# Sample attention of a two-layer decode step: rounds of four column tiles instead of pairs of three

## What is computed

```python
qa = partial_rotary(heads(aq, ATT_HEADS), pos)
k_all = jnp.concatenate([k_past, ka.astype(k_past.dtype)], axis=1)
v_all = jnp.concatenate([v_past, heads(av, ATT_HEADS).astype(v_past.dtype)], axis=1)
o_a = dilated_window_attention(qa, k_all, v_all, k_past.shape[1]).reshape(B, T, -1)
...
k_buf = k_all[:, L - new_len:]
v_buf = v_all[:, L - new_len:]
```

## Time and profile before

| | before |
|---|---|
| median of the runs | 1862.29 us |
| profiled execution | 1861.73 us |
| its span | 1859.9 us |
| PE matmul records | 1780.8 us, 96% of the span |
| VectorE, ScalarE | 46%, 35% |
| mean granted clock of PE | 0.971 |
| attention stage, layer 0 (290.0 to 386.1 us) | 96.1 us, PE 84.57 us busy, DMA share 0.89 |
| attention stage, layer 1 (1212.1 to 1307.2 us) | 95.1 us, PE 84.26 us busy, DMA share 0.89 |

### The profile page before, as it was taken

One profiled execution on the slowest core, in us unless ns is written; L12 is line 12 of the kernel. 1 busy time (PEld: TensorE's weight loads), 2 busy tenths in 40 slices (PEclk: granted clock), 3 DMA queues, 4 the chain that ended last, 5 costly groups with the idle time before them and its releaser, 6 DMA issues.

```text
span 1859.9 us, 35744 instructions
## 1 busy us (share of the span) xinstructions
PE 1780.8 (96%) x16096; PEld 1651.1 (89%) x16096; DVE 863.1 (46%) x1333; ACT 655.8 (35%) x967; POOL 71.0 (4%) x90
## 2 busy tenths in 40 slices
PE   6999998999999999999989999988999999999998
PEld 5988995588999999999979889855989999999988
DVE  5514775445423333345655148854354133333465
ACT  5422324544423222233344322255344231222233
POOL 0012110000000000000000121100000000000000
PEclk9999898999999999999989998989999999999999
DMA  6521418952755626352353223289319366355311
GB/s 262 184 68 54 167 43 330 342 182 80 249 173 198 239 80 225 107 189 80 104 188 124 69 100 110 113 324 341 140 58 331 110 215 218 108 195 178 123 63 63
DMA packets 73960, 303.50 MB, mean 163 GB/s; under 512 B 6096, under 2 KB 28240, under 8 KB 72144
## 3 DMA queue, kind: packets, MB, share of 16 engines
q1 hardware_dynamic: 66384, 200.94, 30.8%
q0 software_dynamic: 7424, 100.27, 15.4%
HBM read 290.57 MB, written 110.89 MB: 216 GB/s over the span
## 4 chain that ended last, share of the span: by engine, by line
PE 89%; DVE 6%; ACT 3%; issue 1%; DMA 0%; DVEq 0%; ACTq 0%
PE pair L1651 15%; PE pair L1653 14%; PE pair L1652 14%; PE pair L864 3%; PE pair L715 3%; PE pair L717 2%; PE pair L719 2%; PE pair L990 2%; PE pair L697 2%; PE pair L647 2%; PE pair L699 2%; PE pair L698 2%; PE pair L970 2%; PE pair L649 2%; PE pair L648 2%; PE pair L1731 2%
## 5 line engine op out<-in xcount | busy, mean ns | idle before, releaser
L1651 PE MATMUL pair<-x_hi_part,w_hi_part 128*128 128x288 f32 x1088 | 322.2, 296 | 2.1 <-DVE tmp L2030 2.1
L1652 PE MATMUL pair<-x_lo_part,w_hi_part 128*128 128x288 f32 x1088 | 321.0, 295 | 0.0
L1653 PE MATMUL pair<-x_hi_part,w_lo_part 128*128 128x288 f32 x1088 | 319.9, 294 | 0.0
L1967 DVE TENSOR_TENSOR w_lo_part<-raw,w_hi_part 128x1024 fp32r<-128x1024 f32 x154 | 188.7, 1226 | 235.6 <-ACT w_hi_part L1818 235.6
L1651 PE MATMUL pair<-u_hi_part,w_hi_part 128*128 128x288 f32 x928 | 274.7, 296 | 0.0
L1652 PE MATMUL pair<-u_lo_part,w_hi_part 128*128 128x288 f32 x928 | 273.8, 295 | 0.0
L1653 PE MATMUL pair<-u_hi_part,w_lo_part 128*128 128x288 f32 x928 | 272.8, 294 | 0.0
L1818 ACT ACTIVATE w_hi_part<-raw 128x1024 fp32r<-128x1024 f32 x154 | 161.8, 1051 | 209.9 <-PE pair L1653 208.3
L1651 PEld LDWEIGHTS pair<-x_hi_part,w_hi_part 128*128 128x128 f32 x1088 | 203.9, 187 | 2.5 <-DVE tmp L2030 2.5
L1653 PEld LDWEIGHTS pair<-x_hi_part,w_lo_part 128*128 128x128 f32 x1088 | 204.9, 188 | 0.0
L1652 PEld LDWEIGHTS pair<-x_lo_part,w_hi_part 128*128 128x128 f32 x1088 | 204.3, 188 | 0.0
(11 more groups left out here) (278 smaller groups left out, 3450.8 us busy)
## 6 DMA issues: line engine op xcount, KB each, us to landing
raw<-w_units SPq DMA_DIRECT2D x210, 512.0 KB, 3.6
ck_out<-ck POOLq DMA_DIRECT2D x16, 3060.0 KB, 14.2
cv_out<-cv POOLq DMA_DIRECT2D x16, 3060.0 KB, 23.2
arena<-cv SPq DMA_DIRECT2D x8, 1920.0 KB, 13.4
tail<-cv SPq DMA_DIRECT2D x8, 1920.0 KB, 10.6
arena<-ck SPq DMA_DIRECT2D x6, 1920.0 KB, 11.7
more<-ck SPq DMA_DIRECT2D x6, 1920.0 KB, 12.1
h<-ck SPq DMA_DIRECT2D x4, 1920.0 KB, 12.2
```

Source lines behind the costliest of these rows:

```text
L1651: nc.tensor.matmul(out, wh[:, cols], xh[:, k, t], start=n == 0, stop=False)
L1652: nc.tensor.matmul(out, wh[:, cols], xl[:, k, t], start=False, stop=False)
L1653: mm = nc.tensor.matmul(out, wl[:, cols], xh[:, k, t], start=False, stop=n == KT - 1)
L1967: return tt_(dst, src, hi.bitcast(F32), ALU.subtract).then_inc(*up(done, 1))
```

## The change

The 12 combinations of a pair of batches and a pair of heads are worked off in three rounds of four column tiles instead of four rounds (pairs) of three, so that 128 rows are filled. Combination 4r + t belongs to pair (4r + t) // 3 and heads (4r + t) mod 3. There are now 12 couples = 3 rounds x 4 slots: slot 0 the output's and the round's transposes (128 columns each), slot 1 both score calls of the next round, slot 2 the first weighing, slot 3 the second. Keys and values are loaded in pieces of one batch and one pair of heads (640 KB), 24 of each, into nine and six buffers. Key piece n waits for score call (n - 9) // 4 + 1, value piece n for weighing (n - 6) // 4 + 1. In SP's order all keys come ahead of value piece 6. Values are laid out in DRAM so that a partition's ten rows of a piece are one run of 5120 bytes; before, a run was 1536 bytes. ScalarE copies the round's transposes in three instructions instead of two; VectorE's copies of the turned output stay four per round. On VectorE and ScalarE `s_max` and `s_exp` of the next round stay in slot 2. The new-position bias has three blocks instead of four. The copy of the value cache to its output takes whole rows of a batch.

```diff
-ROWS = 96
+ROUNDS, ACROSS = 3, 4
+QCOLS = 96
 COLS = KEYS + NEW
+def combination(r, t):
+    return divmod(ACROSS * r + t, 3)
+def piece(n):
+    r, j, t = n // (2 * ACROSS), n // ACROSS % 2, n % ACROSS
+    p, c = combination(r, t)
+    return 2 * p + j, c
+PIECES = 2 * ACROSS * ROUNDS
+KBUF, VBUF = 9, 6
...
-            KB = [area(0, 3 * KEYS, 3), more_sb[:, 0:3 * KEYS].rearrange("p (a t) -> p a t", a=3),
-                  h_sb[:, 0:3 * KEYS].rearrange("p (a t) -> p a t", a=3)]
-            VB = [area(16640, KC * 384, KC), area(9728, KC * 384, KC)]
-            PTB = area(13568, 11 * ROWS, 11)
-            PTP = [area(14624, 512), area(15136, 512)]
+            KB = [v[:, i * KEYS:(i + 1) * KEYS] for v in (arena, more_sb, h_sb) for i in range(3)]
+            VB = [area(o + i * KEYS, KEYS, KC) for o in (9728, 16640) for i in range(3)]
+            PTB = area(13568, 11 * P, 11)
+            PTP = [area(14976, 512), area(21824, 512)]
...
-                def load_keys(b):
-                    sp.dma_start(KB[b % 3], of_layer(ck)[b * 384:(b + 1) * 384, 0:KEYS]
-                                 .rearrange("(c p) n -> p c n", p=P)).then_inc(*up(k_landed[b % 3], 16))
-                def load_values(b):
-                    sp.dma_start(VB[b % 2], of_layer(cv)[b * WIN:b * WIN + KEYS, :]
-                                 .rearrange("(c p) n -> p c n", p=P)).then_inc(*up(v_landed[b % 2], 16))
+                def load_keys(n):
+                    b, c = piece(n)
+                    if n >= KBUF:
+                        sp.wait_ge(*at(ss_mm, (n - KBUF) // ACROSS + 1))
+                    sp.dma_start(KB[n % KBUF], of_layer(ck)[b * 384 + c * P:b * 384 + (c + 1) * P, 0:KEYS]
+                                 ).then_inc(*up(k_landed[n % KBUF], 16))
+                def load_values(n):
+                    b, c = piece(n)
+                    if n >= VBUF:
+                        sp.wait_ge(*at(so_mm, (n - VBUF) // ACROSS + 1))
+                    at_ = (3 * b + c) * WIN
+                    sp.dma_start(VB[n % VBUF].rearrange("p k n -> p (k n)"), of_layer(cv)[at_:at_ + KEYS, :]
+                                 .rearrange("(p k) n -> p (k n)", p=P)).then_inc(*up(v_landed[n % VBUF], 16))
                 sp.wait_ge(*at(lv_ready, len(LEVELS) - 1))
-                load_keys(0)
+                for n in range(3):
+                    load_keys(n)
                 sp.wait_ge(*at(lin_mm, Q[IN2[-1]] + 1))
-                load_keys(1)
-                load_keys(2)
+                for n in range(3, 9):
+                    load_keys(n)
                 sp.wait_ge(*at(lv_mm, len(LEVELS) * len(GROUPS)))
-                load_values(1)
+                for n in range(3):
+                    load_values(n)
                 sp.wait_ge(*at(o_ready, 5))
-                load_values(0)
-                def more_keys(b):
-                    sp.wait_ge(*at(ss_mm, b - 2))
-                    load_keys(b)
-                def more_values(b):
-                    sp.wait_ge(*at(so_mm, b - 1))
-                    load_values(b)
-                for b in (3, 4, 5, 6):
-                    more_keys(b)
-                more_values(2)
-                more_values(3)
-                more_keys(7)
+                for n in range(3, 6):
+                    load_values(n)
+                for n in range(9, 16):
+                    load_keys(n)
+                for n in range(16, PIECES):
+                    load_keys(n)
+                for n in range(6, 10):
+                    load_values(n)
+                for n in range(10, 14):
+                    load_values(n)
                 for r in range(R_OUT, R_OUT + AHEAD):
                     load(sp, r)
-                more_values(4)
-                more_values(5)
+                for n in range(14, 18):
+                    load_values(n)
                 for r in range(R_OUT + AHEAD, R_OUT + RAW):
                     load(sp, r)
...
+                for n in range(18, PIECES):
+                    load_values(n)
...
-                    b = 2 * p + j
-                    pe.wait_ge(*at(k_landed[b % 3], 16 * (b // 3 + 1)))
+                    first = (2 * r + j) * ACROSS
+                    for t in range(ACROSS):
+                        pe.wait_ge(*at(k_landed[(first + t) % KBUF], 16 * ((first + t) // KBUF + 1)))
                     for n, (lo, w) in enumerate(((0, 512), (512, 512), (1024, 256))):
-                        for c in range(3):
-                            mm = nc.tensor.matmul(bank[n][32 * c:32 * c + 32, 0:w], QB[:, b, c, :], KB[b % 3][:, c, lo:lo + w],
-                                             start=j == 0, stop=j == 1)
+                        for t in range(ACROSS):
+                            b, c = piece(first + t)
+                            mm = nc.tensor.matmul(bank[n][32 * t:32 * t + 32, 0:w], QB[:, b, c, :],
+                                                  KB[(first + t) % KBUF][:, lo:lo + w], start=j == 0, stop=j == 1)
                     mm.then_inc(*up(ss_mm, 1))
+                def s_turn(r):
+                    pe.wait_ge(*at(ss_exp, r + 1))
+                    if r >= 1:
+                        pe.wait_ge(*at(os_ev, r))
                     for k in range(KC):
-                        nc.tensor.transpose(bank[2 + k // 5][:, ROWS * (k % 5):ROWS * (k % 5 + 1)],
-                                            SMS[0:ROWS, k * P:(k + 1) * P], IDENT[0:ROWS, 0:ROWS])
-                    nc.tensor.transpose(bank[0][0:NEW, 0:ROWS], SMS[0:ROWS, KEYS:COLS],
-                                        IDENT[0:ROWS, 0:ROWS]).then_inc(*up(sp_mm, 1))
-                def s_weigh(p):
-                    pe.wait_ge(*at(sp_ev, p + 1))
+                        b_, o = (bank[2 + k // 4], P * (k % 4)) if k < 8 else (bank[0], P * (k - 8))
+                        nc.tensor.transpose(b_[:, o:o + P], SMS[:, k * P:(k + 1) * P], IDENT)
+                    nc.tensor.transpose(bank[0][0:NEW, 2 * P:3 * P], SMS[:, KEYS:COLS], IDENT).then_inc(*up(sp_mm, 1))
+                def s_weigh(r, j):
+                    if j == 0:
+                        pe.wait_ge(*at(sp_ev, r + 1))
+                    first = (2 * r + j) * ACROSS
+                    for t in range(ACROSS):
+                        pe.wait_ge(*at(v_landed[(first + t) % VBUF], 16 * ((first + t) // VBUF + 1)))
+                    for k in range(KC):
+                        for t in range(ACROSS):
+                            nc.tensor.matmul(bank[3][32 * t:32 * t + 32, P * j:P * j + P], PTB[:, k, 32 * t:32 * t + 32],
+                                             VB[(first + t) % VBUF][:, k, :], start=k == 0, stop=False)
+                    for t in range(ACROSS):
+                        c = combination(r, t)[1]
+                        mm = nc.tensor.matmul(bank[3][32 * t:32 * t + 32, P * j:P * j + P],
+                                              PTB[0:NEW, KC, 32 * t:32 * t + 32],
+                                              V[0:NEW, TT, 640 + P * c:640 + P * c + P], start=False, stop=True)
+                    mm.then_inc(*up(so_mm, 1))
...
                             s_back(p - 1)
                         s_turn(p)
                     elif slot == 1:
-                        if p + 1 < PAIRS:
+                        if p + 1 < ROUNDS:
                             s_scores(p + 1, 0)
                             s_scores(p + 1, 1)
+                    elif slot == 2:
+                        s_weigh(p, 0)
                     else:
-                        s_weigh(p)
+                        s_weigh(p, 1)
                 weigh(len(COUPLES) - 1)
-                s_back(PAIRS - 1)
+                s_back(ROUNDS - 1)
...
                 def s_turned(p):
                     act.wait_ge(*at(sp_mm, p + 1))
-                    A(PTB[:, 0:KC].rearrange("p (a k) m -> p a (k m)", a=2), pair[1][:, :, 0:5 * ROWS], ACT.Copy)
-                    A(PTB[0:NEW, KC], bank[0][0:NEW, 0:ROWS], ACT.Copy).then_inc(*up(sp_ev, 1))
+                    A(PTB[:, 0:8].rearrange("p (a k) m -> p a (k m)", a=2), pair[1][:, :, :], ACT.Copy)
+                    A(PTB[:, 8:KC].rearrange("p k m -> p (k m)"), bank[0][:, 0:2 * P], ACT.Copy)
+                    A(PTB[0:NEW, KC], bank[0][0:NEW, 2 * P:3 * P], ACT.Copy).then_inc(*up(sp_ev, 1))
...
```

More of the change, by code:

```diff
@@ L121 @@
 C_NBIAS = C_SBIAS + KEYS
-C_SCALE = C_NBIAS + PAIRS * NEW
+C_SCALE = C_NBIAS + ROUNDS * NEW
 C_EPS = C_SCALE + 1
@@ L289, in build @@
         pt_mm, pt_ev = sem("pt_mm"), sem("pt_ev")
-        k_landed, v_landed = [[sem(f"{n}_landed{i}") for i in range(m)] for n, m in (("k", 3), ("v", 2))]
+        k_landed, v_landed = [[sem(f"{n}_landed{i}") for i in range(m)] for n, m in (("k", KBUF), ("v", VBUF))]
         ss_mm, ss_max, ss_exp, ss_p = sem("ss_mm"), sem("ss_max"), sem("ss_exp"), sem("ss_p")
@@ L570, in _ @@
                 sp.dma_start(of_layer(kn_out).rearrange("p (c t) -> p c t", c=3), qk[:, 3:6, SEQ:T]).then_inc(*up(kv_out, 16))
-                for j in range(2):
```

(16 more changed lines are left out.)

115 lines of the change are left out of this document (52 added, 63 removed).

## The result

The changed kernel takes 1907.8 us (median of four runs, 1904.6 to 1911.9), the kernel before beside it 1863.4. The ratio is 1.0235, 95% interval 1.0211 to 1.0259; in a second comparison it was 1.0212 (1.0174 to 1.0249). The forecast of 1882 us had the direction right and somewhat under half the size (+20.5 us where +44.4 were measured), and the measured time lies above its range, which ends at 1897. The profiled execution took 1909.5 us, span 1907.7.

A forecast was written before the change was run, and what follows sets the result against it. PE's matmul work was taken as the bound. Per layer -10.1 + 12.8 + 3.2 + 4.8 = +10.7 us; two layers +21.4, less 0.9 for "issue", gave +20.5 on 1861.7: 1882 us, range 1864 to 1897.

The forecast's parts named there:

- PE's work: Attention stage, per layer: two fewer score calls and weighings, less new-key scoring, slightly cheaper transposes; -10.1 us.
- waits for values: Before each round's second weighing, PE waits for two value pieces whose buffers free late; three waits, +12.8 us per layer.
- lower clock: After each value wait PE works at 1.2 GHz, losing 2.6 us each; net +4.8 us per layer.
- The fourth column tile: Score and weighing calls: four tiles cost what three did, 2.15 and 2.66 us a call.
- the rival wanted 2.7 us or more for four: Fourth tile not free: calls up to 4/3 as long, 1901 us at most, half of it 1892; chance 0.1.
- The wait of round 0: Second weighing of round 0: values queue behind seven key pieces, landing at 332.3 us; PE waits 5.4 us.
- The waits of rounds 1 and 2: Second weighings there: two pieces land in 5.6 us, PE has 2.2 and 1.6 us of work; waits 3.4 and 4.0 us.
- Chain waits: PE's waits for ScalarE and VectorE by prompt couple, 9.3 us before and 12.5 after; +3.2 us per layer.
- The replay: PE, ScalarE, VectorE and queue replayed in program order with trace durations; kernel before ended at 385.8 us, trace 386.1.
- The clock didn't hold: Judges the rival that value waits bring no lower-clock loss afterwards: +2.8 us per layer, 1866 us; chance 0.12.
- the rival with a chance of 0.1: Small pieces land late: each value wait 1 us longer, +3 us per layer, 1888 us; chance 0.1.
- faster, the value waits are hidden: Value pieces land before PE asks for them: -6.9 us per layer, 1847 us; chance 0.07.

The follow-up runs named there:

- the kernel with the slots set anew: Changed kernel, p_out before s_turned, value pieces 6-9 before keys 17-23, first weighing in slot 1, next round's scores in slot 2; 1857.7 us, ratio 0.9962.
- the first pair of profiles: First profiled executions, nothing further changed: kernel before 1861.73 us, changed kernel 1909.5 us.
- second pair of profiles: Both kernels profiled once more, nothing further changed: changed kernel 1900.3 us, kernel before 1855.8 us.
- The kernel before with the pieces alone: Kernel before, with keys and values in three transfers per sample, the new DRAM layout of values and its copy to the output; 1869.3 us, ratio 1.0033.
- the layout alone: Kernel before, with the new DRAM layout of values and its copy to the output, but one large transfer per sample as before; 1864.3 us, ratio 0.9994.

## Why the prediction was wrong

Per layer, against the windows above. The measured share of PE's work is taken from the kernel with the slots set anew, layer 0, as its clock is that of before; the clock's share is what is left of busy time. Both columns are of the first pair of profiles.

| Term | Forecast | Layer 0 | Layer 1 |
|---|---|---|---|
| PE's work | -10.1 | -10.5 | -9.8 |
| waits for values | +12.8 | +16.2 | +16.2 |
| other waits | +3.2 | +3.8 | +6.7 |
| lower clock | +4.8 | +9.8 | +4.7 |
| stage | +10.7 | +19.3 | +17.8 |

Other waits are idle time (+20.0 and +22.9) less 16.2; the profile has no other waits for values than the six, 32.4 us in both layers. In the second pair of profiles the stages are 15.9 and 19.2 us longer and idle time 21.4 and 20.4, so a single entry for idle or busy time is good to some 4 us.

**The fourth column tile, and what PE is relieved of: right.** 2.15 and 2.67 us a call with four tiles. The Trainium skill ("TensorE: Matmul & The Clock Gate", Part 3) has a speed-up of 2.38 for three tiles. No run here has a call of one tile to hold that against; but the rival wanted 2.7 us or more for four, and the measured 2.15 us decide against it.

**The wait of round 0: mis-sized, 7.0 instead of 5.4 us.** PE came 0.6 us later than reckoned, at 329.1 instead of 328.5 (the forecast's 326.9, by its own terms 326.8, and the 1.6 us by which the stage starts later). The nine pieces took longer: from the first key issue of slot 1 to the landing 336.05 - 317.34 = 18.7 us, where 14.4 + 2.5 = 16.9 were reckoned. The mechanism, seven key pieces ahead of two value pieces in the queue, is shown by moving them. SP's timeline, changed kernel, has both issues, and those of pieces 14, 22 and 23 below them:

```profile
317.34 0.33 SPq L554 DMA_DIRECT2D h<-ck  x1
...
324.32 1.28 SPq L562 DMA_DIRECT2D arena<-cv  x3
...
364.18 0.33 SPq L562 DMA_DIRECT2D arena<-cv  x1
...
394.19 0.80 SPq L562 DMA_DIRECT2D tail<-cv  x2
```

**The waits of rounds 1 and 2: 3.55 us for 3.4, and 5.67 for 4.0.** In round 1 the pieces landed 369.84 - 364.18 = 5.7 us after issue, where 5.6 were taken. In round 2 it was 401.41 - 394.19 = 7.2 us. Why it took longer there isn't settled; SP issues the copies of the new values to their outputs right behind these two pieces. The Trainium skill's "Anatomy of one DMA" ("DMA: Bandwidth & Descriptors"), a fit for transfers that GpSimd issues, gives an estimate of 5.0 us for two pieces; these are issued by SyncE, and both landings were longer.

**Chain waits: the step that failed.** The forecast had +3.2 us, from couples 9 to 11 and a wait of 2.3 for VectorE. The latter came (2.2). But of the idle time above the values' in layer 0, 5.2 us are the wait for `p_out`, and the rest fell by 1.4 us, so that the total of +3.8 us is close to the forecast by luck. In layer 1 it is +6.7. The replay had no dependency of `weigh` on `pv_ev`: in the trace of before it never costs anything, so no row shows it, and it stands in the code alone. So the failed step is the couple-by-couple sum of PE's waits for ScalarE: it had 1.1 us each for couples 4 and 8 and nothing for `p_out`, which cost 2.6 us four times, 10.4 us in the run; moving it forward gave back 12.5 us. The prediction followed each step that the change moves; `p_out` is not moved, but the slots are moved under it.

**The clock: mis-sized too.** Forecast: three stretches at the lower level, one behind each value wait, with 2.6 us lost in each. The window of the changed kernel behind and in the first value wait, and three further ones, in layer 0:

```profile
328.10:341.80 13.70, 6.74 (x96) 0.50 0.66 270
348.60:355.40 6.80, 6.32 (x50) 0.50 0.48 195
...
369.10:372.50 3.40, 2.66 (x52) 0.50 1.02 424
382.70:393.00 10.30, 9.18 (x90) 0.50 0.16 67
```

The granted clock is the lower level, 1.2 GHz, for 13.7 us in the first, 6.7 of them with work in them. The second stretch begins at the wait for `p_out` in couple 4, which wasn't in the sum, and the last stands in couples 8 to 9 behind the same wait in couple 8 (381.53). The first and third follow value waits, and half of their work is 4.7 us. But which waits are followed by the lower level differs by execution. The second profile of the changed kernel has the same wait of 2.60 us for `p_out`, ending at 343.30, and the full clock behind it:

```profile
343.00:350.00 7.00, 6.66 (x82) 1.00 0.43 175
```

So these windows don't give `p_out` a price in clock. By the terms of the table the clock cost +9.8 and +4.7 us in the first pair of profiles and, with 10 us for PE's work, some +5 and +9 in the second: 7 us a layer on average, where 4.8 were forecast. That layer 0 lost twice what layer 1 did is one execution's.

**Outside the stages: forecast nothing, 10.7 us in the first pair of profiles.** 47.8 us of span less 37.1 in the stages. 1.8 of it is where the first stage starts, which differs by execution. 7.7 us are the stretch between the stages. The kernel before with the pieces alone has these 7.7 us too, though its waits in the stage are those of before, so they don't come from the longer stage; with the layout alone they are 3.8 us, and in the variants of the changed kernel 2.7 to 7.9. It is busy time at a lower mean clock with the waits of the stretch nearly unchanged. What moves the clock there stays open: the experiments don't separate number of transfers, layout, copy to the output and what happens to fall together. The layout of before wasn't tried on the changed kernel.

**The rivals.** The clock didn't hold; the fourth tile was free; the small pieces landed later than reckoned in two of three places, by 1.8 and 1.6 us, which is the rival with a chance of 0.1. The value waits are 3.4 us a layer longer than forecast, where that rival had +3. The rival "faster, the value waits are hidden", 1847 us, is what the kernel with new slots makes of it: values cost 1.7 us a layer there, and it takes 1857.7.

The range was too narrow because it held nothing for a wait that no row shows: two unlisted costs, the order of two ScalarE steps (some 12 us by experiment) and the stretch between the stages (3 to 9 us), are most of the 26 us above the forecast. The late pieces bring 3.4 us a layer, and what the clock costs above its forecast is in part in these numbers already.

## What to carry to other kernels

When the number of slots of a hand-written order changes, go through every step keyed to a loop index, moved or not, and ask in which slot it now falls and what stands ahead of it there. A wait of the bounding engine can cost more than its length, where the granted clock is lower behind it: here 1.5 to 1.6 times. A share of a few microseconds needs a second profile of the same kernel before it is given a cause: here busy time of the same stage differed by 3.8 us between two. More parallel tiles bring their gain only if the buffers and the queue are a slot ahead of them: the same twelve calls were 2.3% slower or 0.4% faster than the sixteen before, by the order of the steps and loads around them alone.

## What the runs showed of the hardware

Four column tiles of 32 ran as fast as three: 24 records of 512 and 256 columns in 2.15 us against 18, at full clock. The waits of 7.0 and 3.6 us taken away in both layers, 21.2 us, gave back 32.0 to 34.5, of which 10.0 to 12.6 us were the same matmuls at a higher clock. A wait of 2.60 us was followed by a granted clock of 0.50 in one execution and of 1.00 in the next of the same kernel. And the stretch between the stages, with 7030 matmul records in every kernel here, took between 823.5 and 832.7 us.
